# Second input projection: the sum of squares of the recurrence rows two units into the next turn, and its norm's end behind the convolution

## The chip, the cores and the metric

The kernel runs on one core of a Trainium2 chip. The metric is the device time of one execution in microseconds (us). The core has five engines with their own instruction queues: TensorE (PE in the profile, its weight loads PEld), VectorE (DVE), ScalarE (ACT), GpSimd (POOL) and SyncE (SP). An engine works through its queue strictly in order; engines wait for each other by semaphores.

## The reference, cut to what matters

The model has two blocks in a row. The change lies in the second one, where 2048 tokens of width 1024 are normed, modulated and multiplied by one wide matrix. The product is split into latents for an attention and two times 512 columns for a gated linear recurrence:

```
h = rms_norm(x, norm1_g) * (1.0 + scale1) + shift1
proj = h @ w_in
q_lat, kv_lat, k_rope, x_lru, g_lru = jnp.split(proj, IN_SPLITS_2, axis=-1)
...
xc = causal_conv(x_lru, conv_w) + conv_b                # 4 taps
r = sigmoid(xb @ w_a + b_a);  i = sigmoid(xb @ w_x + b_x)   # block diagonal
a = exp(-8 * r * softplus(-lam));  mult = sqrt(max(1 - a*a, 0))
h_t = a_t * h_(t-1) + mult * (i * xc)                   # reset where positions == 0
lru = h * gelu(g_lru)
...
mixed = concat([rms_norm(attn, attn_out_norm), rms_norm(lru, lru_out_norm)])
```

(`causal_conv` and the last lines are abridged.) What the change moves is the last norm of `lru`: for each token the mean over its 512 channels of `lru * lru`, the root of it, its reciprocal, and the product of `lru` with that and with `lru_out_norm`. In this layout the channels lie in the partitions, so the sum over channels is a matmul with a matrix of ones.

## The kernel before, in words

`second_projection` is one stage, with the names `inp_...` in the profile. It works on 256 tokens at a time, called a turn: `turns` runs eight bodies, the first three and the last written out, the four between in a loop of two. In turn g TensorE projects tile g (ten units, u = 0 to 9: eight units of 128 feature columns, of which two share a bank of `psU`, and two token tiles of 448 columns), and `beside(g - 1, u)` puts the attention and recurrence matmuls of the tile before between the units. After the last turn come the same steps of the last tile with nothing beside them, called the tail here.

The engines' queues follow the order of the `body` function of each:

- VectorE in turn g: `finish(g - 2)` (L2980 reciprocal, L2983 four products, the end of the norm), `norm_latents(g - 1)` (L2860 to L2871), `convolve` (L2887, L2889), `mark`, `norm(g + 1)` (L2810 to L2816, the input norm of the next tile), then heads, `decay`, heads, `scan` (L2963 to L2975), the edges of the convolution (L2879) and the copies of the token banks from `psU` to `tm` (L3005).
- ScalarE in turn g: `root_latents` (L3044), `keep_fm` 0 (L3038, frees the first bank of `psU`), `take_latents`, gates 0 and 1 (L3062, L3063), `root(g + 1)` (L3026), `keep_fm` 1, `take_heads` 0, gates 2 and 3, an evacuation of turned input, `head_root` 0 (L3087), and so on to `m_root`, `head_root` 1, `gelu`, `keep_turned` and at the end `norm_root(g - 1)` (L3120, the root of the norm).
- TensorE in turn g: unit 0 waits for `tm_kept`, the token copies of the turn before; `beside` turns the latents and makes gates 0 and 1 behind unit 2, projects heads 0 behind unit 3, makes gates 2 and 3 behind unit 4 (L3226), projects heads 1 behind unit 5, turns heads 0 behind unit 7, and behind unit 9 turns heads 1 and makes the sum of squares (L3256), which waits for `multiplied`, given when `scan` has ended on VectorE.

The small products of a tile go through four banks of `psX` in a fixed order of 21 slots; the sum of squares is the last, `N`. The semaphore `slotted` counts slots filled (21 for each tile) and `slot_kept` slots emptied. `convolve(b)` waits for `slotted` at 21 b, that is until every matmul of the tile before, the sum of squares among them, is done, since it overwrites their operands. The first latents of a tile use the bank of the tile before's `N`, so TensorE waits there until `norm_root` has emptied it.

Of the kernel before, what the change touches and what calls it, by code (L numbers as in the profile page):

```python
# [2657 lines left out]
def second_projection(nc, K, x_in, scale1, shift1, columns_in, positions, pos_row, inv, q_a_norm, kv_a_norm, w_q_b, w_kv_b, q_norm, k_norm,  # L2658
# [22 lines left out]
    with Stage(nc, "inp2") as s:  # L2681
# [65 lines left out]
        def late(g, by=1):  # L2747

            return not isinstance(g, int) or g >= by
# [10 lines left out]
        last = TURNS - 1  # L2760
# [44 lines left out]
        def _(dve):  # L2805
# [178 lines left out]
                                             op0=ALU.mult, op1=ALU.mult).then_inc(final, 1)  # L2984

            def body(g, par, follows):
                if late(g, 2):
                    finish(g - 2)
                if late(g):
                    norm_latents(g - 1)  # L2990
                    convolve(g - 1, 1 - par)
                    mark(g - 1, 1 - par)
                if follows:
                    norm(g + 1)
                if late(g):
                    sum_heads(g - 1, 0)
                    heads(g - 1, 0)
                    decay(g - 1)
                    sum_heads(g - 1, 1)
                    heads(g - 1, 1)  # L3000
                    scan(g - 1)
                edges(g, par)
                for j in range(TB):
                    dve.wait_ge(unit, g * U + NP + j + 1)
                    dve.tensor_copy(tm[:, j, :], psU[:, j, 0:TM2_W]).then_inc(tm_kept, 1)  # L3005
            norm(0)
            set_up()
            turns(dve, body)
            finish(last - 1)
            norm_latents(last)  # L3010
            convolve(last, last % 2)
            mark(last, last % 2)
            for j in range(TB):
                sum_heads(last, j)
                heads(last, j)
                if j == 0:
                    decay(last)
# [4 lines left out]
        def _(act):  # L3022
# [13 lines left out]
            def keep_fm(g, par, m):  # L3036
                act.wait_ge(unit, g * U + m + 1)
                act.activation(fm[:, par, 2 * m:2 * m + 2, TAPS - 1:L], psU[:, m % 2, :].rearrange("p (f t) -> p f t", f=2), ACT.Copy  # L3038
                               ).then_inc(fm_kept, 1)
# [84 lines left out]
            def body(g, par, follows):  # L3124
                if late(g, 2):
                    act.wait_ge(g_ready, g - 1)
                    act.wait_ge(convolved, g * LB - LB)
                b = g - 1
                if late(g):
                    root_latents(b)  # L3130
                keep_fm(g, par, 0)
                if late(g):
                    for j in range(TB):
                        take_latents(b, j)
                    for k in range(2):
                        gate(b, k)
                if follows:
                    root(g + 1)
                keep_fm(g, par, 1)
                if late(g):  # L3140
                    take_heads(b, 0)
                    for k in range(2, 4):
                        gate(b, k)
                if follows:
                    evacuate(g + 1, 1 - par, 0)
                if late(g):
                    head_root(b, 0)
                keep_fm(g, par, 2)
                if late(g):
                    decays(b)  # L3150
                    take_heads(b, 1)
                if follows:
                    evacuate(g + 1, 1 - par, 1)
                    evacuate(g + 1, 1 - par, 2)
                if late(g):
                    m_root(b)
                    head_root(b, 1)
                    gelu(b, 1 - par)
                keep_fm(g, par, 3)
                if follows:  # L3160
                    evacuate(g + 1, 1 - par, 3)
                if late(g):
                    keep_turned(b, 0)
                    keep_turned(b, 1)
                    norm_root(b)

            root(0)
            for q in range(4):
# [7 lines left out]
            act.wait_ge(sch, 7)  # L3176
            act.wait_ge(zeroed, 2)
            turns(act, body)
            root_latents(last)
            for j in range(TB):  # L3180
                take_latents(last, j)
# [16 lines left out]
        def _(pe):  # L3198
# [60 lines left out]
            def beside(b, u):  # L3259

                if u == 2:
                    turn_latents(b, 0)
                    turn_latents(b, 1)
                    gates(b, 0)
                    gates(b, 1)
                if u == 3:
                    project(b, 0)
                if u == 4:
                    gates(b, 2)
                    gates(b, 3)  # L3270
                if u == 5:
                    project(b, 1)
                if u == 7:
                    turn_heads(b, 0)
                if u == 9:
                    turn_heads(b, 1)
                    sum_squares(b)

            def body(g, par, follows):
                pe.wait_ge(hT_ready, g * (2 * TB) + 2 * TB)  # L3280
                for u in range(NF + TB):
# [19 lines left out]
                        mm.then_inc(unit, 1)  # L3301
                    if follows and 4 <= u < 8:
                        turn(g + 1, u - 4)
                    if late(g):
                        beside(g - 1, u)
            for q in range(4):
# [1 line left out]
            pe.wait_ge(columns_in.fm_landed, 32)  # L3308
            pe.wait_ge(fixed, FIXED)
            turns(pe, body)  # L3310
            for u in range(NF + TB):
                beside(last, u)

        @block.gpsimd
        def _(pool):
# [862 lines left out]
```

## Time and profile before

| | us |
|---|---|
| median of 3 runs | 4330.12 (4329.88 to 4331.2) |
| the profiled execution | 4328.15 |
| its span | 4326.5 |
| TensorE busy | 3961.4 (92%) |
| VectorE busy | 1731.6 (40%) |
| ScalarE busy | 1458.8 (34%) |
| GpSimd busy | 589.1 (14%) |
| sums of squares, L3256, x64 matmuls | 17.4, and 13.7 idle before them |
| stage of the second projection | about 2380 to 2925 of the span |

Times within the profile are microseconds from the start of the span.
### The profile page before, as it was taken

How to read it: one execution, taken by the hardware profiler on the slowest of the kernel's cores; microseconds unless marked ns; L12 is line 12 of the kernel's file. 1: busy time of each engine (PE TensorE's matmuls, PEld its weight loads, DVE VectorE, ACT ScalarE, POOL GpSimd, SP SyncE). 2: the span in 40 equal slices, each digit the busy share in tenths (PEclk: the TensorE clock that was granted, in tenths of full speed). 3: DMA queues.
4: the chain of work that ended last, by engine and by line, in shares of the span. 5: the costliest groups of instructions: out<-in, count | busy, mean ns of one | idle time of the engine just before them, and what ended most of it. 6: DMA issues, size and time to landing. Idle time of an engine off the chain costs nothing. (4 is left out here: it accounts for less than half of the span.)

```text
span 4326.5 us, 53728 instructions
## 1 busy us (share of the span) xinstructions
PE 3961.4 (92%) x17976; PEld 2483.8 (57%) x17977; DVE 1731.6 (40%) x3722; ACT 1458.8 (34%) x3219; POOL 589.1 (14%) x747
## 2 busy tenths in 40 slices
PE   6999999799989977999999899969999898799998
PEld 4676676454755535777776677745555454333333
DVE  1343344565545551111101477773333445333332
ACT  1122122455434411111110566652333122344443
POOL 0000000000430011111110000000000001333323
PEclk8999999899989968999999999979999998899999
DMA  6221221222434476565654221122231233688873
GB/s 228 80 77 67 93 87 57 81 88 78 142 109 162 157 267 229 181 209 167 213 164 143 67 64 64 60 87 68 58 97 38 84 121 125 229 288 284 286 209 73
DMA packets 228079, 581.82 MB, mean 134 GB/s; under 512 B 27926, under 2 KB 98982, under 8 KB 212058
## 3 DMA queue, kind: packets, MB, share of 16 engines
q1 hardware_dynamic: 176378, 395.70, 26.3%
q0 software_dynamic: 51552, 184.18, 14.1%
q8 instruction: 88, 1.44, 0.1%
q14 instruction: 61, 0.50, 0.0%
HBM read 437.60 MB, written 142.12 MB: 134 GB/s over the span
## 5 line engine op out<-in xcount | busy, mean ns | idle before, releaser
L2100 PE MATMUL out_psO<-out_w,out_mixT 128*128 128x512 f32 x1024 | 450.1, 598 | 3.3 <-ACT out_mixT L2072 1.8
L878 PE MATMUL inp_psU<-inp_w,inp_hT 128*128 128x512 f32 (+3 forms) x1376 | 420.8, 464 | 0.0
L3927 PE MATMUL moe_psU<-moe_wu,moe_xT 128*64 x768 | 345.7, 604 | 6.2 <-issue 5.4
L3929 PE MATMUL moe_psU<-moe_bu,moe_xT 128*64 128x512 f32 x768 | 345.7, 604 | 0.0
L878 PEld LDWEIGHTS inp_psU<-inp_w,inp_hT 128*128 128x128 f32 x1376 | 256.0, 190 | 152.7 <-issue 122.4
L2100 PEld LDWEIGHTS out_psO<-out_w,out_mixT 128*128 128x128 f32 x1024 | 193.9, 192 | 237.4 <-issue 237.4
L874 PE MATMUL inp_psU<-inp_hT,inp_w 128*128 128x256 f32 x1088 | 243.8, 384 | 9.4 <-DVE inp_tm L680 4.5
L2573 PE MATMUL moe_psG<-moe_xT,moe_g_w 128*128 128x256 f32 x1024 | 233.5, 381 | 4.4 <-DMA moe_u_w<-in_w_up 4.4
L2589 PE MATMUL moe_psD<-moe_d_w,moe_hT 128*128 128x512 f32 x512 | 223.9, 595 | 9.8 <-DVE moe_hT L2632 9.8
L3291 PE MATMUL inp_psU<-inp_hT,inp_w 128*128 128x256 f32 x1024 | 231.3, 382 | 1.8 <-ACT inp_hT L3032 1.8
L874 PEld LDWEIGHTS inp_psU<-inp_hT,inp_w 128*128 128x128 f32 x1088 | 207.7, 193 | 41.3 <-issue 3.9
L2573 PE MATMUL moe_psG<-moe_xT,moe_u_w 128*128 128x256 f32 x1024 | 231.5, 379 | 0.0
L3927 PEld LDWEIGHTS moe_psU<-moe_wu,moe_xT 128*64 128x64 f32 x768 | 102.8, 139 | 211.0 <-issue 211.0
L2613 ACT ACTIVATE moe_sg<-moe_psG 128x256 f32<-128x256 f32 x64 | 24.5, 383 | 575.3 <-PE moe_psG L2573 575.3
L3291 PEld LDWEIGHTS inp_psU<-inp_hT,inp_w 128*128 128x128 f32 x1024 | 195.8, 192 | 35.2 <-issue 9.2
L2573 PEld LDWEIGHTS moe_psG<-moe_xT,moe_g_w 128*128 128x128 f32 x1024 | 192.2, 191 | 35.7 <-issue 7.2
L2573 PEld LDWEIGHTS moe_psG<-moe_xT,moe_u_w 128*128 128x128 f32 x1024 | 194.6, 190 | 26.5
L2632 DVE TENSOR_TENSOR moe_hT<-moe_sg,moe_psG 128x256 f32<-128x256 f32 x64 | 27.0, 421 | 447.2 <-ACT moe_sg L2613 447.2
L3871 POOL DMA_INDIRECT out_rows<-moe_y,moe_at_out x48 | 125.7, 2619 | 367.7 <-DMA out_rows<-moe_y,moe_at_out 181.3
L3905 PE MATMUL moe_psD<-moe_wd,moe_hT 128*64 x384 | 172.7, 592 | 1.3 <-ACT moe_hT L3967 1.3
L3908 PE MATMUL moe_psD<-moe_bd,moe_hT 128*64 128x512 f32 x384 | 172.7, 592 | 0.0
L680 DVE COPY inp_tm<-inp_psU 128x512 f32<-128x512 f32 (+3 forms) x86 | 45.4, 527 | 315.8 <-PE inp_psU L878 315.8
(654 smaller groups left out, 6765.7 us busy)
## 6 DMA issues: line engine op xcount, KB each, us to landing
moe_wu<-in_w_up SPq DMA_DIRECT2D x32, 2048.0 KB, 18.1
moe_g_w<-in_w_gate SPq DMA_DIRECT2D x16, 2048.0 KB, 8.4
moe_u_w<-in_w_up SPq DMA_DIRECT2D x16, 2048.0 KB, 13.3
moe_d_w<-in_w_down SPq DMA_DIRECT2D x16, 2048.0 KB, 10.2
moe_wd<-in_w_down SPq DMA_DIRECT2D x32, 1024.0 KB, 20.0
mod_w<-in_w_ada SPq DMA_DIRECT2D x24, 1024.0 KB, 7.6
inp_mod_w<-in_w_mod SPq DMA_DIRECT2D x16, 1024.0 KB, 4.9
xn<-out_xn POOLq DMA_DIRECT2D x32, 512.0 KB, 3.8
```

Source lines behind the costliest of these rows:

```text
L680: dve.tensor_copy(tm[:, j, at:at + n], psU[:, u % NB, 0:n]).then_inc(tm_kept, by)
L874: mm = pe.matmul(psU[:, u % NB, 0:G], w[:, k, fm_lo + u * P:fm_lo + (u + 1) * P], hT[:, par, k, :], start=(k == 0), stop=(k == KD - 1))
L878: mm = pe.matmul(psU[:, u % NB, 0:n], hT[:, par, k, j * P:(j + 1) * P], w[:, k, lo:lo + n], start=(k == 0), stop=(k == KD - 1))
L2100: mm = pe.matmul(psO[:, j, h, :], mixT[:, j, k, :], out_weights.half[k // 4][:, k % 4, h * BANK:(h + 1) * BANK], start=(k == 0), stop=(k = ...
L2573: mm = pe.matmul(psG[:, f % 2, at_col:at_col + N], w[:, j, k, f * P:(f + 1) * P], xT[:, p, k, :], start=(k == 0), stop=(k == KD - 1))
L2589: mm = pe.matmul(psD[:, b, :], hT[:, f, r * P:(r + 1) * P], d_w[:, j, f, h * BANK:(h + 1) * BANK], start=(f == 0), stop=(f == FB - 1))
L3291: mm = pe.matmul(psU[:, m % 2, u % 2 * G:(u % 2 + 1) * G], w[:, k, TM2_W + u * P:TM2_W + (u + 1) * P], hT[:, par, k, :], start=(k == 0), s ...
L3871: pool.indirect_dma_start(out=out, out_offset=bass.IndirectOffsetOnAxis(ap=at_out[:, p, :], axis=0), in_=y[:, p, :], in_offset=None, compu ...
L3905: pe.matmul(psD[0:HALF, n, :], hT[:, p, f, 0:HALF], wd[:, bass.ds(slot, 1), f, c].rearrange("p a n -> p (a n)"), start=(f == 0), stop=(f = ...
L3908: mm = pe.matmul(psD[HALF:P, n, :], hT[:, p, f, HALF:P], bd[:, p, f, c], start=(f == 0), stop=(f == FB - 1), tile_position=(0, HALF))
L3927: pe.matmul(psU[0:HALF, p, :], xT[:, p, k, 0:HALF], wu[:, bass.ds(slot, 1), k, :].rearrange("p a n -> p (a n)"), start=(k == 0), stop=(k = ...
L3929: mm = pe.matmul(psU[HALF:P, p, :], xT[:, p, k, HALF:P], bu[:, p, k, :], start=(k == 0), stop=(k == KD - 1), tile_position=(0, HALF))
```

## The change

The sum of squares of tile g - 2 is made by TensorE in turn g, behind unit 1, instead of in turn g - 1 behind unit 9. ScalarE's `norm_root` of it comes behind `keep_fm` 0 of turn g instead of at the end of turn g - 1. VectorE's `finish(g - 2)` stays in turn g but moves from the front to behind `mark`. At the end of the program's stage the three follow in the same way.

```
 # VectorE
             def body(g, par, follows):
-                if late(g, 2):
-                    finish(g - 2)
                 if late(g):
                     norm_latents(g - 1)
                     convolve(g - 1, 1 - par)
                     mark(g - 1, 1 - par)
+                if late(g, 2):
+                    finish(g - 2)
                 if follows:
                     norm(g + 1)
...
             turns(dve, body)
-            finish(last - 1)
             norm_latents(last)
             convolve(last, last % 2)
             mark(last, last % 2)
+            finish(last - 1)
...
 # ScalarE
                 keep_fm(g, par, 0)
+                if late(g, 2):
+                    norm_root(b - 1)
...
                     keep_turned(b, 1)
-                    norm_root(b)
...
             turns(act, body)
+            norm_root(last - 1)
             root_latents(last)
...
 # TensorE
                 if u == 9:
                     turn_heads(b, 1)
-                    sum_squares(b)
...
+                    if late(g, 2) and u == 1:
+                        sum_squares(g - 2)
                     if late(g):
                         beside(g - 1, u)
...
             turns(pe, body)
+            sum_squares(last - 1)
             for u in range(NF + TB):
                 beside(last, u)
+            sum_squares(last)
```

## Rows read from the trace of the kernel before

**Rows 1.** Waits, 2380 to 2925: who waited for whom, total us, times, longest.

```profile
DVE inp_nrm L2980 <- ACT inp_nrm L3120: 17.0, 8, 5.8
...
PE inp_psX L3256 <- DVEq L2976: 13.7, 7, 5.5
```

**Rows 2.** Busy time in stretches: a middle turn, and the tail.

```profile
core 0: us, PE busy (x) PEld busy (x) DVE busy (x) ACT busy (x) POOL busy (x), PEclk, DMA share, GB/s
...
2681.00:2742.00 61.00, 59.58 (x259) 44.75 (x258) 46.43 (x108) 40.39 (x81) 4.14 (x6) 1.00 0.19 62
...
2860.00:2925.00 65.00, 25.57 (x78) 17.20 (x78) 44.24 (x101) 31.45 (x59) 5.21 (x7) 0.62 0.45 132
```

**Rows 3.** Timeline of TensorE, turn 5: both of its boundaries and unit 4's gates.

```profile
2679.92 1.96 PE L3256 MATMUL inp_psX<-inp_r,ones 128*128 128x256 f32 x8 [1.43 <-DVEq L2976]
2681.72 10.52 PE L3291 MATMUL inp_psU<-inp_hT,inp_w 128*128 128x256 f32 x48
...
2706.36 1.89 PE L3226 MATMUL inp_psX<-inp_xc,inp_wg 128*128 128x256 f32 x8
...
2740.29 1.97 PE L3256 MATMUL inp_psX<-inp_r,ones 128*128 128x256 f32 x8 [1.42 <-DVEq L2976]
```

**Rows 4.** Timeline of VectorE and ScalarE in the same turn.

```profile
2680.06 1.16 DVE L3005 COPY inp_tm<-inp_psU 128x448 f32<-128x448 f32 x2
...
2682.43 1.75 DVE L2980 RECIPROCAL inp_nrm<-inp_nrm 128x256 f32<-128x256 f32 x1 [1.22 <-ACT inp_nrm L3120]
2684.22 1.68 DVE L2983 SCALAR_TENSOR_TENSOR inp_lo<-inp_lo,inp_small,inp_nrm 128x256 f32<-128x256 f32 x4
...
2689.83 0.41 DVE L2887 TENSOR_SCALAR inp_xc<-inp_fm,inp_cw,inp_small 128x256 f32<-128x256 f32 x1
...
2697.91 1.22 DVE L2810 CUSTOM_DVE_ANT_0 inp_xsq<-inp_x 128x1024 f32<-128x1024 f32 x1
...
2700.44 0.29 ACT L3026 ACTIVATE inp_st<-inp_st,eps 128x1 f32<-128x1 f32 x1 [0.97 <-DVE inp_st L2810]
...
2704.82 1.28 ACT L3062 ACT_TABLE_LOAD   x1
...
2707.42 0.47 ACT L3062 ACTIVATE inp_r<-inp_psX,inp_small 128x256 f32<-128x256 f32 x1 [1.32 <-PE inp_psX L3226]
...
2725.77 0.28 ACT L3087 ACTIVATE inp_hs<-inp_hs,eps 128x8 f32<-128x8 f32 x1
```

**Rows 5.** Timeline, turn 3: unit 0 and ScalarE's gates 2 and 3.

```profile
2559.57 10.52 PE L3291 MATMUL inp_psU<-inp_hT,inp_w 128*128 128x256 f32 x48
...
2586.60 0.47 ACT L3062 ACTIVATE inp_r<-inp_psX,inp_small 128x256 f32<-128x256 f32 x1 [1.32 <-PE inp_psX L3226]
```

**Rows 6.** Timeline, turn 7: VectorE's first work behind its mark.

```profile
2825.58 0.95 DVE L2905 TENSOR_REDUCE inp_hs<-inp_hsq 128x4 f32<-128x768 f32 x1 [6.90 <-ACT inp_hsq L3083]
```

**Rows 7.** Timeline, the start of the tail.

```profile
2857.72 1.15 DVE L3005 COPY inp_tm<-inp_psU 128x448 f32<-128x448 f32 x2
...
2860.96 0.47 ACT L3120 ACTIVATE inp_nrm<-inp_psX,eps 128x256 f32<-128x256 f32 x1
...
2864.85 0.42 DVE L2860 CUSTOM_DVE_ANT_0 inp_junk<-inp_tm 128x256 f32<-128x256 f32 x1
...
2868.32 1.53 PE L3219 MATMUL inp_psX<-ident,inp_tm 128*128 128x128 f32 x6 [8.73 <-DVE inp_tm L2871]
...
2881.68 0.95 DVE L2905 TENSOR_REDUCE inp_hs<-inp_hsq 128x4 f32<-128x768 f32 x1 [4.77 <-ACT inp_hsq L3083]
```

**Rows 8.** Idle gaps of TensorE in other stages, and what followed them.

```profile
3267.26 1.46 PE L3499 MATMUL lata_psO<-inp_w,lata_pT 128*128 128x128 f32 x8 [2.30 <-DVE lata_o L3544]
3268.52 3.31 PE L3470 MATMUL lata_psS<-lata_kn,lata_qn 128*128 128x512 f32 x4
...
3272.82 1.77 PE L3470 MATMUL lata_psS<-lata_kn,lata_qn 128*128 128x512 f32 x4
...
3832.92 0.44 PE L3938 MATMUL moe_psH<-ident,moe_h 128*128 128x128 f32 x2 [3.42 <-DVE moe_h L4016]
...
3836.00:3838.00 2.00, 2.00 (x8) 0.69 (x6) 0.00 (x0) 2.00 (x5) 1.22 (x2) 0.50 1.02 434
```

More of the change, by code:

```diff
@@ L2986, in body @@
             def body(g, par, follows):
-                if late(g, 2):
-                    finish(g - 2)
                 if late(g):
@@ L2992, in body @@
                     mark(g - 1, 1 - par)
+                if late(g, 2):
+                    finish(g - 2)
                 if follows:
@@ L3008, in _ @@
             turns(dve, body)
-            finish(last - 1)
             norm_latents(last)
@@ L3012, in _ @@
             mark(last, last % 2)
+            finish(last - 1)
             for j in range(TB):
@@ L3131, in body @@
                 keep_fm(g, par, 0)
+                if late(g, 2):
+                    norm_root(b - 1)
                 if late(g):
@@ L3164, in body @@
                     keep_turned(b, 1)
-                    norm_root(b)
             root(0)
@@ L3178, in _ @@
             turns(act, body)
+            norm_root(last - 1)
             root_latents(last)
@@ L3276, in beside @@
                     turn_heads(b, 1)
-                    sum_squares(b)
             def body(g, par, follows):
@@ L3303, in body @@
                         turn(g + 1, u - 4)
+                    if late(g, 2) and u == 1:
+                        sum_squares(g - 2)
                     if late(g):
@@ L3310, in _ @@
             turns(pe, body)
+            sum_squares(last - 1)
             for u in range(NF + TB):
                 beside(last, u)
+            sum_squares(last)
         @block.gpsimd
```

## The prediction

> **What bounds the kernel now.** The page's busy table comes first: TensorE is busy for 92% of the span, so what moves the time is a gap of TensorE or work ahead of one. The waits view of this stage [rows 1] says where TensorE stops: seven times before the sum of squares (L3256), 13.7 us together, the longest 5.5; and VectorE itself stands 17.0 us, eight times, before the norm's reciprocal (L2980) for ScalarE. The stage makes eight turns. A turn in the middle keeps TensorE busy for nearly all of its 61 us at the full clock; the last turn's own attention and recurrence work, with no projection beside it, is 65 us at a mean clock of 0.62 [rows 2]. So there are two places: the boundary between turns and the tail.
>
> Then the timeline of one turn, unit 0 at 2681.72 [rows 3]. TensorE stood 1.43 us until VectorE had ended its scan, ran the sum of squares from 2679.92 (1.80 us until the projection starts), and the next sum of squares starts at 2740.29, 58.6 us after unit 0. TensorE idles there, so the last link of the turn is not TensorE. I followed it back on the other engines [rows 4]. ScalarE runs from the gates of heads 2 and 3 (2707.42) to the second head root (2725.77), some 18 us, with no idle time reported in front of any instruction; VectorE takes over there (heads, scan, product). And the gates at 2707.42 had waited 1.32 us for TensorE's unit 4, whose gate matmuls start at 2706.36. The cycle of a turn is therefore: unit 0, TensorE to unit 4, ScalarE for 18 us, VectorE's last 14 us, sum of squares, unit 0. The only cover that I find for a later ScalarE is that 1.32 us.
>
> **The change part by part.** All times are from unit 0 of that turn.
>
> *The sum of squares leaves the boundary.* Before, unit 0 comes 1.80 us behind the end of VectorE's product. Afterwards it must still wait for VectorE's copy of the first token bank (tm_kept): 2680.06 and half of 1.16, about 2680.65, and some 0.15 to hand over (my allowance), so 2680.8 instead of 2681.72 [rows 3, 4]: 0.9 us earlier, not 1.80 plus 1.43. Six boundaries (before turns 2 to 7): -5.4. Bounds: 0 if the copy were held up, -10.8 if it cost nothing.
>
> *It comes back two units later.* 32 of the 48 matmuls that take 10.52 us are 7.0 us; then the sum of squares is 1.8 to 1.96 us, ending at +8.9. VectorE's convolution waits for it (slotted), because a turn's slot count now ends there; it started at 2689.83, +8.1 [rows 4]. So +0.8 us, though the latents ahead of it start 4.5 us sooner. They gain nothing: TensorE wants them only behind unit 2. TensorE reaches unit 4 1.8 us later.
>
> *The norm's end moves behind the convolution.* Convolution and mark take 8.1 us (2689.83 to 2697.91), now ending at +17.0; then reciprocal and four products, 1.75 + 1.68 = 3.4 us, then the next tile's norm, which started at +16.2 and now starts at +20.4: 4.2 us late [rows 4]. ScalarE has the roots of that norm in its queue ahead of the third copy of the projection, the copies of heads 0 and the gates 2 and 3. The second root ended at 2700.73 (+19.0), now +23.2; what stands between it and the table load of the gates is 4.1 us, the load 1.28: the gates can start at +28.6. TensorE's unit 4 has them ready at about +27.5. They started at +25.7. So ScalarE's long stretch is 2.9 us late, and with it the scan: 4.2 less the 1.32 of cover. Four turns (2, 4, 5, 6) pay this: +11.6. Turn 3 is different: its gates already start at 27.03 us behind unit 0 (2559.57 to 2586.60) [rows 5], because the norm came late there, and that delay lies where VectorE will now wait anyway; 28.6 less 27.0 is +1.6. In turn 7 there is no next tile: VectorE waited 6.90 us for heads 0 [rows 6], which hides the 3.4; only the 1.8 of the sum of squares ahead of unit 2 counts, +1.8. Bounds of one ordinary turn: 1.8 (TensorE's delay alone, if ScalarE caught up) to 4.2 (no cover).
>
> *ScalarE.* norm_root moves next to root_latents; both use the square root, so the count of table loads stays, and it runs at about +9.5 in time that ScalarE spent waiting for the latents. Nothing. POOL's store of the recurrence rows moves with the finish to about +20.4, still in front of the stores of v and of the turned tiles in its queue; who waits for it is the product at the end of the scan, 36 us later, and for v the next turn's heads: also free.
>
> *The tail.* Before: the token copies end at 2858.87, VectorE waits for the norm (its root ran from 2860.96, 0.47 us), finishes, and starts the latents at 2864.85; TensorE resumes at 2868.32 after 8.73 us idle [rows 7]. Afterwards the latents start at 2858.9, their squares are done when ScalarE ends the norm root at 2861.43; the root of the latents follows, 0.3, reciprocal and scaling 0.8, and TensorE resumes at about 2862.65. That is -5.7. The finish then costs 3.4 us of VectorE behind the mark, from about 2871.2 (2863.1 and the 8.1 of convolution and mark) to 2874.6; its next work waited 4.77 us until 2881.68, or about 2876 afterwards. It is covered by 1.4 us. If TensorE gets faster here, by no more.
>
> Sum without the clock: -5.4 + 11.6 + 1.6 + 1.8 - 5.7 = +3.9.
>
> *The clock.* TensorE's idle time at a boundary becomes 1.43 + 2.9 + 0.9 - 1.8 = 3.4 us, at five boundaries (before turns 3 to 7). Before turn 2 it is 2.1. Idle gaps of this size are rare in the trace [rows 8]. After 3.42 us the first matmuls run at full speed, and 3 us after they start the granted clock reads 0.50. After 2.30 us four 128x512 matmuls took 3.31 us, where the same four took 1.77 shortly behind: half speed, 1.5 us lost, and some more in the eight small matmuls ahead of them (I use 1.7). None of the 1.43 us gaps of this stage did that: the middle turns read 1.00. A drop in units 0 and 1 delays the sum of squares, the convolution and all behind it, so it passes whole into the turn. So each of five boundaries costs between 0 and 1.7 us, 0 to 8.5 together; I take three of five, +5.0, as the nearest row (3.42) does drop but the gaps fall differently each time. In the tail the gap shrinks from 8.7 to 3.1 us, and part of what ran at half speed runs faster: -0.9 (0 to -1.5).
>
> The row says that such a gap may cost or not. The Trainium skill's "TensorE: Matmul & The Clock Gate", section "HAM oscillation — how this bites in real kernels", describes a wait that recurs in every round of a loop and pays the fall of the clock every single time. By that all five would pay, and the sum would be +11.5 and not +8.0; it is rival B below, and it speaks against the change.
>
> In all +3.9 + 5.0 - 0.9 = +8.0 us. The profiled execution took 4328.15 us (span 4326.5), which gives 4336.2; the median of the runs lies 2.0 above it, at 4330.12, so I name 4338.1. What a measurement of this kernel can tell from no change is about 0.2%, 8.7 us: my forecast ends just inside.
>
> **Rivals.** A: the clock holds. Then +3.9 less the tail's 0 to 1.5 us, some +3.3: 4333.4. For it: the 3.42 gap resumed at full speed, and TensorE is busy without a break on both sides of each gap. Against: half a clock did follow there, and once after a shorter gap. B: every gap costs its 1.7: +3.9 + 8.5 - 0.9 = +11.5: 4341.6. C, faster: ScalarE isn't the link. If the 4.2 us by which the next tile's norm is late stayed under the cover (that is, if they were less than 1.3 us, or the 18 us had slack that the rows don't show), the turns would be TensorE's own: the idle time in front of six sums of squares goes, 13.7 less the 5.5 of the last one = 8.2, and 5.7 of the tail: -13.9, 4316.2. For it: TensorE is 97% busy in a turn; against: no idle time in that stretch of ScalarE, and VectorE behind it waits for ScalarE. It decides at a lateness of 1.3 us, and I find 4.2. D: the turns cost the 2.9 but later work gives it back in part (ScalarE's stretch isn't pinned to the scan, the evacuations for the next tile have room): half of 11.6, no drops: -2.5, 4327.6.
>
> **How the numbers follow.** Forecast (two to four drops) 0.46; A 0.20; B 0.18; C 0.07; D 0.09. Slower by over 0.2% needs +8.7: nearly all of B and somewhat over two fifths of the forecast's share, with a little of A for work that I priced too low: 0.40. Faster by over 0.2% is C and a part of D: 0.09. The rest, 0.51, is within. The range takes in the forecast with its own spread (+4 to +12), A, B and the upper part of D, and leaves C: 4328 to 4345.
>
> **What would show it.** Right: in the waits view no row L3256 behind L2976 but that of the last turn; instead TensorE idles 3 to 4 us before L3291 for VectorE's token copy (L3005), five times; the distance from unit 0 to unit 0 in turns 4 to 6 is 62 to 64.5 us instead of 60.4; VectorE waits about 4 us before the convolution; the gates' 1.32 us wait of ScalarE is gone; the gap ahead of the tail's latents is about 3 us; the granted clock in turns 3 to 7 is under 1.00. Wrong: turns of 59 us, or no idle time of TensorE between turns (C); turns of 62.4 us at a clock of 1.00 (A); a tail that is not at least 5 us shorter.

## The result: about 11 us slower, where 8 was forecast, inside the range

| | before | after |
|---|---|---|
| median of 9 runs each, side by side | 4331.33 (4329.88 to 4335.47) | 4344.11 (4336.99 to 4351.59) |
| the profiled execution | 4328.15 | 4346.81 |
| its span | 4326.5 | 4345.2 |
| mean granted clock | 0.956 | 0.953 |
| first projection unit of turn 0 to the next stage's first scores | 530.4 | 542.2 |
| from there to the start of the last stage | 795.7 | 796.0 |
| last stage | 605.2 | 611.6 |

The ratio after to before is 1.0026, with a 95% interval of 1.0017 to 1.0035: slower by 7 to 15 us (the two medians lie 12.8 apart), against a forecast of +8.0. The spans differ by more, 18.7 us. The last three rows of the table, read off the timeline, say where: 11.8 us in the stage that was changed, and 6.4 in the last one, whose code is the same. By the other traces, below, this last part is most likely not the change's.

**The waits after,** 2380 to 2945: engine, line waited for, total us, times, longest.

```profile
DVE inp_xc L2887 <- PE inp_psX L3258: 38.3, 6, 7.4
```

The same view for TensorE alone:

```profile
PE inp_psU L3292 <- DVE inp_tm L3005: 18.2, 6, 3.3
...
PE inp_psX L3258 <- DVEq L2976: 5.5, 1, 5.5
PE inp_psX L3221 <- DVE inp_tm L2871: 3.2, 1, 3.2
```

Against [rows 1]: the sum of squares (L3256, now L3258) waits once instead of seven times, and 8.2 us are gone. In their place TensorE waits 18.2 us, six times, before the first unit of a turn (L3292), and VectorE waits 38.3 us before the convolution (L2887), which it never did before. Before the last latents TensorE stands 3.2 us and not the 8.73 of [rows 7].

**The turns after.** Busy time in stretches: turns 2, 3 and 5; the column behind POOL is the granted clock, then the DMA share and GB/s.

```profile
2497.00:2560.00 63.00, 60.39 (x254) 45.48 (x254) 45.95 (x106) 40.77 (x82) 4.38 (x6) 0.97 0.20 61
2560.00:2622.00 62.00, 58.73 (x254) 44.29 (x254) 46.27 (x107) 40.71 (x82) 4.13 (x6) 1.00 0.19 62
...
2686.00:2751.00 65.00, 61.53 (x254) 46.27 (x254) 46.51 (x109) 40.48 (x82) 4.05 (x6) 0.95 0.18 58
```

A turn that took 60.4 us at 1.00 [rows 2] takes up to 64.8 at 0.95. The count of matmuls is no larger (254 against 259): the work is the same, and part of it runs at half the clock.

**The boundaries after.** Timeline of TensorE: the first two units of turns 2 to 7 (one row each), turn 5's sum of squares, and the tail.

```profile
2497.55 8.83 PE L3292 MATMUL inp_psU<-inp_hT,inp_w 128*128 128x256 f32 x32 [2.11 <-DVE inp_tm L3005]
...
2560.95 7.17 PE L3292 MATMUL inp_psU<-inp_hT,inp_w 128*128 128x256 f32 x32 [3.02 <-DVE inp_tm L3005]
...
2622.96 8.86 PE L3292 MATMUL inp_psU<-inp_hT,inp_w 128*128 128x256 f32 x32 [3.28 <-DVE inp_tm L3005]
...
2686.57 9.98 PE L3292 MATMUL inp_psU<-inp_hT,inp_w 128*128 128x256 f32 x32 [3.19 <-DVE inp_tm L3005]
...
2696.39 1.89 PE L3258 MATMUL inp_psX<-inp_r,ones 128*128 128x256 f32 x8
...
2751.38 10.00 PE L3292 MATMUL inp_psU<-inp_hT,inp_w 128*128 128x256 f32 x32 [3.28 <-DVE inp_tm L3005]
...
2816.22 9.99 PE L3292 MATMUL inp_psU<-inp_hT,inp_w 128*128 128x256 f32 x32 [3.29 <-DVE inp_tm L3005]
...
2875.85 1.89 PE L3258 MATMUL inp_psX<-inp_r,ones 128*128 128x256 f32 x8
...
2880.93 1.53 PE L3221 MATMUL inp_psX<-ident,inp_tm 128*128 128x128 f32 x6 [3.19 <-DVE inp_tm L2871]
...
2922.70 3.75 PE L3258 MATMUL inp_psX<-inp_r,ones 128*128 128x256 f32 x8 [5.51 <-DVEq L2976]
...
2937.63 3.75 PE L3475 MATMUL lata_psS<-inp_w 128*128 128x512 f32 x4 [11.18 <-PEq L74]
```

Two things are to be read here. The starts stand 63.40, 62.01, 63.61, 64.81 and 64.84 us apart (the first unit of turn 1 is at 2438.55, 59.00 before); in the kernel before it was 60.11, 61.71, 60.44, 60.38 and 60.43 (and 59.93). And the same 32 matmuls take 7.17 us at the full clock (the row at 2560.95) but 8.83, 8.86, 9.98, 10.00 and 9.99 elsewhere: 1.66, 1.69, 2.81, 2.83 and 2.82 us too long, 11.8 together. I call that the clock's loss. Taken off, the turns are 59.00, 61.74, 62.01, 61.92, 62.00 and 62.01.

**The clock around the boundary of turn 5,** windows of 2 us, columns as above:

```profile
2683.00:2685.00 2.00, 0.38 (x4) 0.14 (x2) 1.90 (x2) 1.31 (x4) 0.00 (x0) 1.00 0.00 0
2685.00:2687.00 2.00, 0.43 (x1) 0.43 (x2) 1.77 (x4) 1.26 (x1) 1.03 (x1) 0.61 0.14 43
2687.00:2689.00 2.00, 2.00 (x6) 1.55 (x6) 1.72 (x11) 0.59 (x2) 0.00 (x0) 0.50 1.01 291
2689.00:2691.00 2.00, 2.00 (x7) 1.55 (x6) 1.86 (x11) 0.00 (x0) 0.00 (x0) 0.50 0.20 59
2691.00:2693.00 2.00, 2.00 (x8) 1.65 (x7) 0.19 (x1) 0.00 (x0) 0.00 (x0) 0.68 0.00 0
2693.00:2695.00 2.00, 2.00 (x11) 1.77 (x10) 0.00 (x0) 0.00 (x0) 0.00 (x0) 1.00 0.00 0
```

TensorE went idle at 2683.38. The clock fell to 0.50 (1.2 GHz) inside the gap: 0.61 over the 2 us from 2685 puts the fall at about 2685.4, before the turn's first matmul at 2686.57. It stayed there until about 2692.3 (0.68 over the 2 us from 2691), so for the first 5.7 us of work: 6 and 7 matmuls in 2 us instead of 11. Half of that is the 2.8 lost.

The boundaries that lost 1.7 look different. Turn 2, first matmul at 2497.55:

```profile
2496.00:2498.00 2.00, 0.45 (x2) 0.40 (x3) 1.75 (x5) 0.36 (x1) 1.00 (x1) 0.93 0.00 0
2498.00:2500.00 2.00, 2.00 (x6) 1.64 (x5) 1.83 (x11) 1.16 (x1) 0.02 (x1) 0.50 0.68 199
2500.00:2502.00 2.00, 2.00 (x8) 1.63 (x7) 1.85 (x10) 0.61 (x3) 0.00 (x0) 0.72 0.67 195
```

Here the clock fell at about 2497.7, just behind the first matmul, and was back at about 2501.1: 3.4 us at half speed, and half of that lost. In turn 4 it fell at about 2624.0 (0.75 over the 2 us from 2623), a microsecond behind the first matmul, again for 3.4 us; in turn 3 it did not fall at all.

**Turn 5 after, VectorE and ScalarE,** to be held against [rows 4]; take 2.81 us, the clock's loss, off every distance from 2686.57.

```profile
2685.89 1.16 DVE L3005 COPY inp_tm<-inp_psU 128x448 f32<-128x448 f32 x2
...
2698.31 0.41 DVE L2887 TENSOR_SCALAR inp_xc<-inp_fm,inp_cw,inp_small 128x256 f32<-128x256 f32 x1 [7.12 <-PE inp_psX L3258]
...
2706.40 1.75 DVE L2980 RECIPROCAL inp_nrm<-inp_nrm 128x256 f32<-128x256 f32 x1
...
2709.77 1.22 DVE L2810 CUSTOM_DVE_ANT_0 inp_xsq<-inp_x 128x1024 f32<-128x1024 f32 x1
...
2712.30 0.29 ACT L3026 ACTIVATE inp_st<-inp_st,eps 128x1 f32<-128x1 f32 x1 [0.97 <-DVE inp_st L2810]
...
2717.73 0.47 ACT L3062 ACTIVATE inp_r<-inp_psX,inp_small 128x256 f32<-128x256 f32 x1
...
2735.95 0.28 ACT L3087 ACTIVATE inp_hs<-inp_hs,eps 128x8 f32<-128x8 f32 x1
```

The first unit starts 0.68 us behind the start of the token copy instead of 1.66. The convolution is at +11.74, less 2.81: +8.9 (before +8.1). The next tile's norm is at +23.20, less 2.81: +20.4 (before +16.2). The gates are at +31.16, less 2.81: +28.35 (before +25.7), with no wait in front. From the gates to the second head root it is 18.22 us (before 18.35).

### The profile page after: what moved, and what is told of

It is laid out like the page before. It is cut to its first block and busy times, and to the rows that moved or that the text cites. A ratio compares the mean times of both kernels' runs of the same rounds, so it can differ in the third digit from the quotient of the medians.

```text
span 4345.2 us, 53728 instructions
## 1 busy us (share of the span) xinstructions
PE 3974.4 (91%) x17976; PEld 2493.3 (57%) x17977; DVE 1732.6 (40%) x3722; ACT 1459.4 (34%) x3219; POOL 590.2 (14%) x747
## 3 DMA queue, kind: packets, MB, share of 16 engines
q8 instruction: 88, 1.44, 0.1%
## 5 line engine op out<-in xcount | busy, mean ns | idle before, releaser
L3292 PE MATMUL inp_psU<-inp_hT,inp_w 128*128 128x256 f32 x1024 | 243.5, 395 | 19.9 <-DVE inp_tm L3005 18.2
L874 PE MATMUL inp_psU<-inp_hT,inp_w 128*128 128x256 f32 x1088 | 243.7, 384 | 9.1 <-DVE inp_tm L680 4.5
L3292 PEld LDWEIGHTS inp_psU<-inp_hT,inp_w 128*128 128x128 f32 x1024 | 202.8, 199 | 57.6 <-issue 15.0
## 6 DMA issues: line engine op xcount, KB each, us to landing
moe_wu<-in_w_up SPq DMA_DIRECT2D x32, 2048.0 KB, 18.2
```

The costliest lines, as they stand in the source:

```text
L874: mm = pe.matmul(psU[:, u % NB, 0:G], w[:, k, fm_lo + u * P:fm_lo + (u + 1) * P], hT[:, par, k, :], start=(k == 0), stop=(k == KD - 1))
L3292: mm = pe.matmul(psU[:, m % 2, u % 2 * G:(u % 2 + 1) * G], w[:, k, TM2_W + u * P:TM2_W + (u + 1) * P], hT[:, par, k, :], start=(k == 0), s ...
```

## The experiments

The theory going in: the turn is a loop through TensorE's first units, the sum of squares, VectorE's convolution and norm, ScalarE's gates and VectorE's scan, lengthened by about 1.5 us, and TensorE's longer idle gap costs the rest in clock. The rivals: the clock is a bystander and the longer chain costs everything; or either the sum of squares or the finish alone is to blame. The medians of the kernel before beside them were 4331.93, 4330.94 and 4331.76 in three sessions. One caution for the texts below: they take the full-clock time of units 0 and 1 as 7.0 us and so count 12.8 us lost; by the rows it is 7.17, and the loss 11.8.

**e1: the clock held.** The changed kernel, with matmuls of no use in the gap, into a bank of psX that is free then.

```
 # TensorE, body
                 pe.wait_ge(hT_ready, g * (2 * TB) + 2 * TB)
+                if late(g, 2):
+                    fill = free(g - 2, "N")
+                    for n in range(6 if late(g, 3) else 4):
+                        pe.matmul(fill[:, 0:G], K["ones"][:, :],
+                                  w[:, 0, 0:G], start=True, stop=True)
                 for u in range(NF + TB):
```

> The changed kernel, with filler for TensorE at the boundary between turns: ahead of unit 0 of turns 2 to 7, before its wait for the token copy, TensorE multiplies the ones matrix with a constant block of weights (4 products of 256 columns in turn 2, 6 in turns 3 to 7, 0.43 us each) into the bank that the sum of squares overwrites later. Results are untouched, the wait for the token copy stays. Theory (the clock): in the changed kernel's trace units 0 and 1 took 8.8, 7.2, 8.9, 10.0, 10.0, 10.0 us in turns 2 to 7 instead of 7.0, 12.8 us together; with the gap of 3.3 us filled to under 1 us the clock stays at full speed, each takes 7.0, the turns are 61.5 to 62.0 us and the kernel is 8 to 13 us faster than the changed one: 4331 to 4335, within 2 us of the one before (+5 from the chain, -6 from the tail, +1.5 in turn 7). Rival (the lost time is the chain's, and the clock only shows idle time): units 0 and 1 get faster but unit 0 to unit 0 stays at 63.4 to 64.8, and the time stays at 4341 to 4347. Second rival (filler matmuls stand in the way): turns get longer by the filler that exceeds the gap, and the time rises above 4346.

Measured: 4333.91, ratio 1.0005 (0.9996 to 1.0014). Timeline of TensorE, turns 5 to 7:

```profile
2683.90 7.17 PE L3296 MATMUL inp_psU<-inp_hT,inp_w 128*128 128x256 f32 x32 [0.57 <-DVE inp_tm L3005]
...
2807.76 7.17 PE L3296 MATMUL inp_psU<-inp_hT,inp_w 128*128 128x256 f32 x32 [0.57 <-DVE inp_tm L3005]
```

The turns are 61.98 and 61.88 us (turn 6 starts at 2745.88), within 0.15 us the turns of the changed kernel with the clock's loss taken off, and all six starts take 7.17. So the chain is what it was, and the loss is the clock's alone. Filling the gap gave the slowdown back, within the interval. This rules out the rival in which the clock is a bystander.

**e2: VectorE's part alone.** The kernel before, with the finish behind `mark` in the body and in the tail; the sum of squares and its root stay where they were.

```
 # VectorE, body (and the same two moves behind turns)
-                if late(g, 2):
-                    finish(g - 2)
                 if late(g):
                     norm_latents(g - 1)
                     convolve(g - 1, 1 - par)
                     mark(g - 1, 1 - par)
+                if late(g, 2):
+                    finish(g - 2)
```

> The kernel before, with only VectorE's part of the change: the norm's end of tile g - 2 behind convolution and mark, in the turns and in the tail; sum of squares and its root where they were. Theory (the end of the norm costs only because the sum of squares holds the convolution back): here the convolution starts some 4.5 us sooner, so the next tile's norm, behind the 3.4 us of the finish, still starts about 1 us sooner than before (+15.1 instead of +16.2 behind unit 0); ScalarE waits for TensorE's gates as before, turns 4 to 6 stay at 60.4 us, turn 3 loses its late gates (-1.3), the tail is 5.7 to 6.5 us shorter: 4331.3 - 7.5 = 4323.8 (ratio 0.9983). Rival (the finish behind the mark is what costs, wherever the sum of squares is): 3.4 us of VectorE in front of the next norm delay the gates by 2 us in each of five turns, +10 and -6: about 4335. Rival C of the prediction (the turns are TensorE's own) expects -6 in the tail and nothing else: 4325.

Measured: 4324.71, ratio 0.9987 (0.9977 to 0.9996): faster than before. Its middle turn, VectorE:

```profile
2676.78 1.16 DVE L3005 COPY inp_tm<-inp_psU 128x448 f32<-128x448 f32 x2
...
2681.99 0.41 DVE L2887 TENSOR_SCALAR inp_xc<-inp_fm,inp_cw,inp_small 128x256 f32<-128x256 f32 x1
...
2690.07 1.75 DVE L2980 RECIPROCAL inp_nrm<-inp_nrm 128x256 f32<-128x256 f32 x1
...
2693.43 1.22 DVE L2810 CUSTOM_DVE_ANT_0 inp_xsq<-inp_x 128x1024 f32<-128x1024 f32 x1
```

and ScalarE:

```profile
2703.89 0.47 ACT L3062 ACTIVATE inp_r<-inp_psX,inp_small 128x256 f32<-128x256 f32 x1 [1.32 <-PE inp_psX L3226]
```

The convolution starts 5.35 us behind the sum of squares (2676.64) with no wait, where before it was 9.91 (2679.92 to 2689.83) [rows 3, 4]; so the finish behind it does no harm, the norm is even 1.2 us sooner (16.8 behind the sum of squares, before 18.0), and the gates wait for TensorE's unit 4 as before. The sums of squares stand 60.1 us apart. The moved finish costs nothing while the convolution isn't held. What holds it is the sum of squares. Most of the gain is the tail's: from the first unit of turn 1 to the first of the tail's two sums of squares the trace is 2.8 us shorter than before, and from there to the next stage 5.4.

**e3: the tail alone.** The kernel before with the last four calls on VectorE in the changed order.

```
 # VectorE, behind turns
-            finish(last - 1)
             norm_latents(last)
             convolve(last, last % 2)
             mark(last, last % 2)
+            finish(last - 1)
```

> The kernel before, with only the tail's edit on VectorE: finish(last - 1) behind the last mark; all turns as before. Theory: the gap ahead of the tail's first transposes shrinks from 8.7 to about 3.2 us and the stage ends 6.1 us sooner, as the changed kernel's tail did (46.9 us from sum of squares to sum of squares instead of 53.0): 4325.2, ratio 0.9986. Rival (3.4 us of VectorE come back later in the tail, since it is VectorE's and ScalarE's there): the gain is 2 to 3 us, 4329.

Measured: 4327.25, ratio 0.9990 (0.9981 to 0.9999). TensorE in the tail:

```profile
2861.38 1.53 PE L3219 MATMUL inp_psX<-ident,inp_tm 128*128 128x128 f32 x6 [3.19 <-DVE inp_tm L2871]
...
2903.06 3.75 PE L3256 MATMUL inp_psX<-inp_r,ones 128*128 128x256 f32 x8 [5.51 <-DVEq L2976]
```

From the first of the tail's two sums of squares (2856.30) to the second it is 46.76 us; before it was 52.99, in the changed kernel 46.85. So the tail gives 6.2 us, and gives them by itself: nothing of it hangs on the turns. The medians show 4.7 of them, with an interval from almost 0 to 8; the theory's 4325.2 and the rival's 4329 lie about equally far off, and it is the trace that decides between them.

**e4: the finish behind the next norm.** The changed kernel with the body's finish one step further back.

```
 # VectorE, body
-                if late(g, 2):
-                    finish(g - 2)
                 if follows:
                     norm(g + 1)
+                if late(g, 2):
+                    finish(g - 2)
```

> The changed kernel, with the norm's end in the turns one step later on VectorE: behind the next tile's input norm instead of ahead of it (the tail as in the changed kernel). Theory (ScalarE's roots of the next input norm hold back gates 2 and 3): they come 3.4 us sooner, the gates' start is TensorE's again (about 27.4 us behind unit 0 where the clock holds, 28.2 in the changed kernel), so a turn is 0.8 us shorter; TensorE's gap at the boundary is 2.5 instead of 3.3 us and some of the clock's 12.8 us go as well: 4334 to 4341, at most as fast as the kernel before. Rival (the place of the finish is indifferent; only the sum of squares ahead of unit 2 and the clock cost): like the changed kernel, 4341 to 4347.

Measured: 4331.70, ratio 1.0004 (0.9995 to 1.0013). TensorE at the starts of turns 4, 5 and 6:

```profile
2618.11 8.86 PE L3292 MATMUL inp_psU<-inp_hT,inp_w 128*128 128x256 f32 x32 [2.33 <-DVE inp_tm L3005]
...
2680.77 7.17 PE L3292 MATMUL inp_psU<-inp_hT,inp_w 128*128 128x256 f32 x32 [2.25 <-DVE inp_tm L3005]
...
2741.82 7.17 PE L3292 MATMUL inp_psU<-inp_hT,inp_w 128*128 128x256 f32 x32 [2.33 <-DVE inp_tm L3005]
```

and ScalarE's gates of turn 5:

```profile
2708.05 0.47 ACT L3062 ACTIVATE inp_r<-inp_psX,inp_small 128x256 f32<-128x256 f32 x1 [1.31 <-PE inp_psX L3228]
```

The gates are at +27.3 and wait for TensorE again: ScalarE's road is off the path, and what remains is the 1.6 us by which TensorE itself comes later to unit 4, for the sum of squares ahead of it. The turn is 61.05 us, 0.65 over before: 1.6 less the 0.93 of the boundary. The gap shrinks to 2.0 to 2.3 us, and the clock's loss falls to 1.66 and 1.69, twice in six. The time came out below the 4334 to 4341 expected: by the trace only 3.4 us of the clock's loss were left.

**A second session: the changed kernel again,** without an edit, to see how firm the losses are.

> The changed kernel once more, for a second trace and more times. Theory: the part that is the same in every execution is the chain, and the part that differs is the clock. Turns less the excess of their units 0 and 1 over 7.0 us are again 61.6 to 62.0 us (the first trace: 61.6, 61.8, 61.8, 61.8, 61.8 for turns 2 to 6), the tail from sum of squares to sum of squares 46.8 us; the excess itself may be anything from 3 to 15 us in all. The 6 to 7 us that the first trace lost in the last stage, beyond this one, were that execution's own: here the rest of the program is within 3 us of the kernel before, or differs in another place. The median 4340 to 4347. Rival: the losses of the clock fall in the same turns with the same sizes, because they follow from the program; then units 0 and 1 read 8.8, 7.2, 8.9, 10.0, 10.0, 10.0 again.

Measured: 4349.15, ratio 1.0042 (1.0029 to 1.0056). The first two units of turns 2, 3 and 5:

```profile
2498.66 7.14 PE L3292 MATMUL inp_psU<-inp_hT,inp_w 128*128 128x256 f32 x32 [2.10 <-DVE inp_tm L3005]
...
2560.37 8.86 PE L3292 MATMUL inp_psU<-inp_hT,inp_w 128*128 128x256 f32 x32 [3.01 <-DVE inp_tm L3005]
...
2688.80 10.04 PE L3292 MATMUL inp_psU<-inp_hT,inp_w 128*128 128x256 f32 x32 [3.19 <-DVE inp_tm L3005]
```

The boundary with 2.1 us of gap lost 1.66 in the first trace and nothing in this one; that with 3.0 lost nothing and now 1.69; the four of 3.2 to 3.3 lost 2.8 each, all but one (1.69, in the first trace). Together 13.1 us, against 11.8. So the same boundary of the same program can lose differently from one execution to another. With that goes the changed kernel's spread over 14.6 us in the first comparison, where the kernel before had 5.6; but the five runs of the second session lie within 4.2. With the losses taken off, the turns of the two traces agree within 0.03 us: the chain is fixed and the clock is not.

The median is above the expected 4340 to 4347. The stage took 544.7 us in this trace, 15 more than in the second trace of the kernel before (below); the medians differ by 18.2, and where the other 3 us lie isn't shown.

**e8: the sum of squares one unit sooner.** The changed kernel with the sum of squares behind unit 0.

```
 # TensorE, body
-                    if late(g, 2) and u == 1:
+                    if late(g, 2) and u == 0:
                         sum_squares(g - 2)
```

> The changed kernel with one size changed: the sum of squares behind unit 0 instead of behind unit 1. Theory (in the changed kernel the convolution stands until the sum of squares is done, 4 us in an undisturbed turn, and all behind it on VectorE and ScalarE with it): it is released at +5.4 us instead of +8.8 behind unit 0, ScalarE reaches gates 2 and 3 3.4 us sooner and waits for TensorE again, whose unit 4 is as late as in the changed kernel; a turn takes 61.0 to 61.1 us where the clock holds, as in e4_behind_norm, TensorE's gap is 2.3 us, the excess of units 0 and 1 is 0 to 6 us in all: 4329 to 4336. Rival (only what TensorE does ahead of unit 4 counts, and that is the same): like the changed kernel, turns of 61.8 us and gaps of 3.3 us, 4340 to 4347.

Measured: 4333.97, ratio 1.0007 (0.9998 to 1.0016). TensorE at turns 5 and 7 (one unit, 16 matmuls), and the gates of turn 5:

```profile
2685.18 3.72 PE L3292 MATMUL inp_psU<-inp_hT,inp_w 128*128 128x256 f32 x16 [2.23 <-DVE inp_tm L3005]
...
2807.30 5.37 PE L3292 MATMUL inp_psU<-inp_hT,inp_w 128*128 128x256 f32 x16 [2.34 <-DVE inp_tm L3005]
```

```profile
2712.46 0.47 ACT L3062 ACTIVATE inp_r<-inp_psX,inp_small 128x256 f32<-128x256 f32 x1 [1.32 <-PE inp_psX L3228]
```

The convolution came at +5.5 in turn 5 (2690.67), the gates at +27.3 with their wait back, the turn at 61.05 us: exactly e4's turn by the other road. Whether the sum of squares comes sooner or the finish later, ScalarE leaves the path at the same point. The clock took 1.7 us three times in six, at gaps of 2.0 to 2.3.

**e6: the loop shortened.** VectorE's moves of e2, gates 2 and 3 made one unit sooner, and on ScalarE the first head root ahead of an evacuation and the decays ahead of the third copy of the projection.

```
 # TensorE, beside
                 if u == 3:
                     project(b, 0)
-                if u == 4:
                     gates(b, 2)
                     gates(b, 3)
 # ScalarE, body
-                if follows:
-                    evacuate(g + 1, 1 - par, 0)
                 if late(g):
                     head_root(b, 0)
-                keep_fm(g, par, 2)
+                if follows:
+                    evacuate(g + 1, 1 - par, 0)
                 if late(g):
                     decays(b)
+                keep_fm(g, par, 2)
+                if late(g):
                     take_heads(b, 1)
```

> The kernel before with VectorE's part of the change (as in e2_finish), and the gates of heads 2 and 3 earlier: on TensorE behind unit 3 instead of unit 4 (the slots keep their order), on ScalarE the first head root ahead of the evacuation of the next tile, and the third copy of the projection behind the decays, so that nothing in ScalarE's long stretch waits for a later unit. Theory (the turn is the loop from TensorE's gates 2 and 3 over ScalarE's stretch and VectorE's scan back to the sum of squares; TensorE's own work is 59.0 us of its 60.1 to 60.4): the loop gets 1.3 to 2.4 us shorter, more than the 1.43 us that TensorE idles, so the idle time ahead of the sum of squares goes to 0 to 0.3 us in turns 1 to 6 and a turn takes 58.7 to 59.1 us: 1.3 us less than e2_finish in six turns, 4324.7 - 8 = 4317 (ratio 0.9968). Rival (ScalarE's stretch has waits of its own that come to the front once the gates are early, the copies of heads 1 above all, whose matmuls stay behind unit 5): half of it, 4321. Rival C of the prediction (the turns were TensorE's own already): no change against e2_finish, 4324.7.

Measured: 4315.87, ratio 0.9964 (0.9950 to 0.9977). Windows over two turns, columns as above:

```profile
2673.00:2732.00 59.00, 59.00 (x256) 44.57 (x257) 46.44 (x109) 40.73 (x83) 3.95 (x5) 1.00 0.20 64
2732.00:2790.00 58.00, 58.00 (x254) 43.83 (x252) 45.83 (x106) 39.74 (x80) 3.93 (x5) 1.00 0.15 47
```

The turns are 58.5 to 58.7 us with TensorE busy without a break: now they are TensorE's own, and it waits for neither of the two copies made later. That is the state that rival C describes, and it needed the slow engines' loop to become shorter than TensorE's 58.7 us; the change had made it longer. By the trace 11.4 us come from the turns and 5.9 from the tail (what e3 gets alone); the medians show 15.1 in all.

**e7: e6 with the tail filled** in the same way, 6, 10, 19, 11 and 20 matmuls of no use into psT at its five waits.

```
 # TensorE, behind turns (fill(n): n matmuls of ones and 256 columns of wkv)
+            before_unit = {2: 6, 7: 10, 9: 19}
             for u in range(NF + TB):
+                fill(before_unit.get(u, 0))
                 beside(last, u)
...
                     turn_heads(b, 1)
+                    if isinstance(b, int) and b == last:
+                        fill(11)
                     sum_squares(b)
...
+                if u == 9:
+                    fill(20)
```

> As e6_gates, and filler for TensorE in the idle gaps of the tail: products of the ones matrix with 256 columns of a fixed weight (0.43 us each at full speed) into a bank of psT that nobody reads any more, 6 ahead of the latents, 10 ahead of the turned heads 0, 19 ahead of heads 1, 11 ahead of the last sum of squares, 20 behind it. Theory (what the tail and the first scores of the next stage lose at half the clock is lost on the chain): the last sum of squares takes 1.9 instead of 3.75 us, the latents 0.8 instead of 1.5, the gates 2.1 instead of 3.7, the turned heads 1.0 instead of 2.0, the first four score matmuls of the next stage 1.8 instead of 3.75; 3 to 7 us less than e6_gates. Rival (the filler runs into the work, since it cannot be interrupted, or the tail is VectorE's and ScalarE's alone): 0 to 2 us less, or slower.

Measured: 4311.25, ratio 0.9952 (0.9938 to 0.9965), the fastest of all kernels here, some 20 us under the one before. TensorE in the tail:

```profile
2886.94 1.87 PE L3254 MATMUL inp_psX<-ident,inp_nope 128*128 128x128 f32 x8 [2.17 <-DVEq L2945]
2895.27 1.97 PE L3261 MATMUL inp_psX<-inp_r,ones 128*128 128x256 f32 x8 [0.38 <-DVEq L2976]
...
2908.41 1.95 PE L3480 MATMUL lata_psS<-inp_w 128*128 128x512 f32 x4 [2.54 <-PEq L74]
```

The last sum of squares takes 1.97 us instead of 3.75, the next stage's first scores 1.95 instead of 3.75. The heads at 2886.94, behind 2.17 us of idle time that the fill left open, still took 1.87 (those at 2875.03 took 1.09). The gain over e6 is 4.6 us by the medians; the intervals of the two overlap.

**A third session: e9, the shortened loop alone.** The kernel before with e6's TensorE and ScalarE edits and none of VectorE's.

> The kernel before with only the gates' edit of e6_gates (gates of heads 2 and 3 behind unit 3 on TensorE; on ScalarE the first head root ahead of the evacuation and the third copy of the projection behind the decays); the norm's end stays at the front of VectorE's turn. Theory: ScalarE reaches the gates at +24.4 us behind unit 0 instead of 25.7, 1.3 us sooner, about the 1.43 us that TensorE idles at the boundary: turns of 59.1 us, idle time ahead of the sum of squares 0.1 to 0.3 us, the tail as before: -7.5 us, 4323.5 (ratio 0.9982). Rival (the edit needs VectorE's part too, which starts the next norm sooner): 2 to 4 us, 4328.

Measured: 4325.52, ratio 0.9986 (0.9976 to 0.9995). The turns are 59.2 to 60.2 us, where 59.1 was expected, with no idle time before the sum of squares and small waits before gates 2 and 3 (TensorE's timeline):

```profile
2690.24 1.13 PE L3227 MATMUL inp_psX<-inp_xc,inp_wg 128*128 128x256 f32 x4 [0.36 <-DVE inp_xc L2889]
```

With the finish at the front the convolution now comes too late for gates made a unit sooner. e2 gives 7.2 us by the medians, e9 6.2, both together (e6) 15.1.

**The kernel before again.** Without an edit.

> The kernel before once more, for a second trace of it, since both traces of the changed kernel took 611.6 and 612.1 us from the first matmul of the last stage to the end of the span and the one of the kernel before took 605.2. Theory (the last stage has a spread of its own, some 605 to 612 us, whatever the second projection does; e2_finish had 606.4, e3_tail 609.1): anything between 605 and 612, and the second projection as in the first trace, 530 us from its first unit to the next stage's first scores. Rival (a later start of the last stage costs it 6 us): 605 again, and the changed kernel's +18.7 us of the first trace are all its doing.

Measured: 4329.79; its last stage took 609.2 us, where the first trace had 605.2, and its changed stage 529.7 (530.4). Of the eleven traces beside the first, ten have 609.0 to 612.4 in the last stage, whatever the kernel (e2's has 606.4). So the 6.4 us that the last stage adds to the difference of the profiled spans most likely belong to a low execution of the kernel before, and not to the change. What makes that stage vary stays open.

## Why the prediction was right or wrong

Direction and range were right: 4344.1 within 4328 to 4345, by one microsecond. That edge was luck: four of the nine runs, and all five of the second session (4347.6 to 4351.7), lie above it. The chances leaned to a change within 0.2% (0.51); the +0.26% that came had 0.40. The term that was mis-sized is the clock's, +5.0 where 11.8 and 13.1 were measured; next to it a part of the chain was too dear by 1.8 us, which hid some of that. For the stage, from the first unit of turn 1 on, in the first trace (13.0 us; it is 11.8 from turn 0 on, since the 80 matmuls at the start of turn 0, which the change doesn't touch, took 19.13 us and in the trace of before 20.37):

| step | predicted | measured |
|---|---|---|
| unit 0 behind the token copy's start | 0.9 sooner | 0.98 sooner (1.66 to 0.68) |
| convolution | +8.9 | +8.9 |
| next tile's norm | +20.4 | +20.4 |
| gates 2, 3 | +28.6, 2.9 late | +28.35, 2.65 late |
| ordinary turn, net of the boundary | +2.0 | +1.6 (turns 2, 4, 5, 6) |
| turn 3, net | +0.7 | +0.3 |
| turn 1, net | -0.9 | -0.9 |
| turn 7 | +1.8 | +1.6 |
| tail, its clock with it | -6.6 | -6.1 |
| chain, all of it | +3.0 | about +1.2 |
| clock in units 0 and 1 | +5.0 | +11.8 (second trace +13.1) |
| sum | +8.0 | +13.0 |

*The boundary and what goes back.* Right to 0.1 us. The sum of squares left the boundary, but not its 1.80 nor its 1.43 us: VectorE's copy of the tokens was close behind.

*The sum of squares ahead of the convolution.* Right, and by e2 it is the root of it: without it the same finish behind the same mark costs nothing.

*The 4.2 us against a cover of 1.32.* Right in its form: the norm is 4.2 late, the wait of [rows 4] gone. The size was 0.25 too large in the gates, as the third copy and the copies of heads 0, between the second root and the table load, took 3.84 us and not 4.1. e4 and e8 lie on the other side of the point at which ScalarE takes over: there the turn is 61.05, by TensorE's own 1.6.

*Turn 7, turn 3, the tail.* As forecast within 0.5 us. The tail's finish at 2889.44 begins as the convolution's mark ends, and VectorE's wait behind it shrank from 4.77 us [rows 7] to 0.80: the cover held, narrowly.

*The clock.* Here the forecast failed, in size and in number. Size: I took 1.7 us a drop from a 2.30 us gap [rows 8], but at gaps of 3.2 to 3.3 the loss was 2.8 in seven cases of eight: in turn 5 the clock fell within the gap and stayed at 0.50 for 5.7 us of the work behind it. The row of a 3.42 us gap that resumed at full speed was a poor neighbour. Number: three of five was allowed and none at the sixth; five of six lost something, in both traces. My bound of 8.5 for all of it was too low, and the sixth boundary was taken as free on the word of its 2.1 us.

Rival B was the nearest as a mechanism, and its 4341.6 is nearer to the median than my 4338.1. The Trainium skill's "TensorE: Matmul & The Clock Gate", section "HAM oscillation — how this bites in real kernels", has the wait in a loop pay each time. The traces agree for the gaps over 3 us, where nine of ten paid. They don't for those of 2.0 to 2.3, where six of fourteen did (after, its repeat, e4 and e8).

Rival A is refuted by the rows at 0.50 and by e1, which is rival A made real: with the clock held the program is at 1.0005. Rival C is refuted by the turns themselves, 62 us with 3 us of idle time in front, and e6 shows what turns that are TensorE's own look like. Rival D, in which later work gives half of the lateness back, didn't come: the gates are 2.65 late, and less the 0.98 of the boundary that is, within 0.1, the 1.6 by which a turn is longer, in the changed kernel and in e1.

Not tried: the sum of squares and its root moved while the finish stays at the front. By the code VectorE would there wait for a root that stands in ScalarE's queue behind the root of the latents, which waits for VectorE: neither would go on. Open is also what decides when the clock falls, inside the gap, behind the first matmuls or not at all, and so why a gap of 3 us costs nothing and the same gap 1.7 in another execution.

## What to carry to other kernels

Before a step is moved off a boundary, follow what its new place stands in front of on each engine: here eight matmuls two units into a turn held the convolution, and three calls later ScalarE's gates, and the loop through the slow engines, not TensorE, set the turn. Price a longer idle gap of TensorE by what the first matmuls behind it may lose, with every gap of the loop at the full loss as the upper bound, or keep the engine at work in it: 34 products of no use gave back some 10 us between the medians (e1 against the first comparison). Where a gap stands at each turn of a loop, shorten the slower engines' way through the turn (e6, -15 us with the tail's share) before moving what happens to lie at the gap.

## What the runs showed of the hardware

- Gaps of 3.19 to 3.29 us lost 2.8 to 2.9 us in the 7.17 us of work behind them seven times in eight, and 1.69 the eighth time; gaps of 3.01 and 3.02 lost 1.69 and nothing; gaps of 1.99 to 2.34 lost 1.65 to 1.69 six times and nothing eight times. The losses come in steps, not in proportion to the gap: in the first trace the clock was at half for 3.4 us behind the first matmul where 1.7 was lost (turns 2 and 4), and for 5.7 us of work where 2.8 was (turn 5).
- Gaps of 1.23 to 1.44 us at the boundaries of the kernel before and of e2 left the clock at 1.00.
- The fall can lie inside the gap: 0.61 over the 2 us from 2685, where a fall at the first matmul would have left 0.89.
